# Turned probabilities copied ahead of the next exponentials, in four attention stages of one fused kernel

## What is computed

```
p = softmax(scale * q k^T [+ mask])      # over the keys
o = p v
```

## Time and profile before

| what | value |
|---|---|
| median of three runs | 4049.82 us |
| the profiled execution, its own time | 4044.61 us |
| its span (first to last instruction) | 4042.6 us |
| TensorE (PE) matmuls busy | 3677.2 us, 91% |
| VectorE (DVE) busy | 1608.9 us, 40% |
| ScalarE (ACT) busy | 1214.8 us, 30% |
| DMA | 76 GB/s over the span |
| mean granted TensorE clock | 0.947 of 2.4 GHz |
| the four attention stages | 614 to 648, 1278 to 1491, 1646 to 1680, 3359 to 3572 us |

### The profile page before, as it was taken

The page is one execution under the profiler, slowest core; times in us unless marked ns, Lnnn a source line. Parts: engine busy times, 40 slices in busy tenths (PEclk is TensorE's granted clock), DMA queues, the critical chain, the costliest instruction groups (busy, mean ns, idle before and its releaser), DMA issues. The chain is left out here.

```text
span 4042.6 us, 44686 instructions
## 1 busy us (share of the span) xinstructions
PE 3677.2 (91%) x17866; PEld 2787.5 (69%) x17866; DVE 1608.9 (40%) x2661; ACT 1214.8 (30%) x2127; POOL 169.1 (4%) x282
## 2 busy tenths in 40 slices
PE   7879798999999989999987999799999888888999
PEld 5448677778665667778866745488887645666777
DVE  5343334333403543343334532344433435544443
ACT  3122224222213542332233110322222435533222
POOL 0033010100000001010000000000000011000000
PEclk9779899999999979999998999899999999998999
DMA  3325331222311003122220201111112300011222
GB/s 147 137 108 226 115 125 63 84 83 104 118 42 42 1 11 125 63 84 87 100 101 31 93 0 42 42 63 62 62 52 94 127 21 22 1 42 63 83 73 104
DMA packets 30052, 307.72 MB, mean 76 GB/s; under 512 B 3843, under 2 KB 5604, under 8 KB 9157
## 3 DMA queue, kind: packets, MB, share of 16 engines
q1 hardware_dynamic: 29894, 305.52, 20.3%
HBM read 303.41 MB, written 2.10 MB: 76 GB/s over the span
## 5 line engine op out<-in xcount | busy, mean ns | idle before, releaser
L561 PE MATMUL psum<-operand_rounded,weights_rest 128*128 128x512 f32 (+1 forms) x1360 | 522.3, 384 | 59.7 <-DVE operand_rest L532 59.7
L562 PE MATMUL psum<-operand_rounded,weights_rounded 128*128 128x512 f32 (+1 forms) x1360 | 519.5, 382 | 0.0
L563 PE MATMUL psum<-operand_rest,weights_rounded 128*128 128x512 f32 (+1 forms) x1360 | 518.8, 381 | 0.0
L530 DVE TENSOR_TENSOR weights_rest<-ring,weights_rounded 128x1024 fp32r<-128x1024 f32 x170 | 208.3, 1225 | 579.2 <-ACT operand_rounded L513 579.2
L326 PE MATMUL psum<-operand_rounded,weights_rest 128*128 128x512 f32 (+1 forms) x1056 | 379.7, 360 | 53.2 <-DVE weights_rest L345 53.1
L327 PE MATMUL psum<-operand_rounded,weights_rounded 128*128 128x512 f32 (+1 forms) x1056 | 377.7, 358 | 0.0
L512 ACT ACTIVATE weights_rounded<-ring 128x1024 fp32r<-128x1024 f32 x170 | 180.1, 1059 | 634.7 <-PE psum L563 567.6
L561 PEld LDWEIGHTS psum<-operand_rounded,weights_rest 128*128 128x128 f32 x1360 | 262.3, 193 | 112.5 <-issue 53.2
L563 PEld LDWEIGHTS psum<-operand_rest,weights_rounded 128*128 128x128 f32 x1360 | 262.0, 193 | 48.2
L562 PEld LDWEIGHTS psum<-operand_rounded,weights_rounded 128*128 128x128 f32 x1360 | 262.3, 193 | 47.6
L326 PEld LDWEIGHTS psum<-operand_rounded,weights_rest 128*128 128x128 f32 x1056 | 200.6, 190 | 90.6 <-issue 60.8
(11 more groups left out here) (430 smaller groups left out, 6155.0 us busy)
## 6 DMA issues: line engine op xcount, KB each, us to landing
ring<-in_ff_w SPq DMA_DIRECT2D x32, 2048.0 KB, 7.7
ring<-in_w_mod SPq DMA_DIRECT2D x24, 2048.0 KB, 7.7
ring<-in_ffn_up SPq DMA_DIRECT2D x22, 2048.0 KB, 7.7
ring<-in_ffn_down SPq DMA_DIRECT2D x33, 1024.0 KB, 4.8
ring<-in_a_w_in SPq DMA_DIRECT2D x4, 2048.0 KB, 11.5
ring<-in_xa_wk SPq DMA_DIRECT2D x4, 2048.0 KB, 7.6
ring<-in_xa_wv SPq DMA_DIRECT2D x4, 2048.0 KB, 7.7
ring<-in_xa_wq SPq DMA_DIRECT2D x4, 2048.0 KB, 7.7
```

Source lines behind the costliest of these rows:

```text
L530: dve.tensor_tensor(parts["weights_rest"][:, r % 2, :], weight_rows(s, r), parts["weights_rounded"][:, r % 2, :].bitcast(F32), ALU.subtrac ...
L561: nc.tensor.matmul(k.bank(m, n), rest, top_in, start=first, stop=False)
L562: nc.tensor.matmul(k.bank(m, n), top, top_in, start=False, stop=False)
L563: mm = nc.tensor.matmul(k.bank(m, n), top, rest_in, start=False, stop=last)
```

## The change

In all four stages ACT's queue in step s takes `copy_turned` first and `exponentials(s)` after it. MLA (`paired`) turns, copies and uses the values one unit later than before (`lag` 3 instead of 2); the cross attentions keep their lag of 2. In the sparse attention, units whose two branches fit one bank together (256 and 128 keys) are turned into one bank and copied by one instruction; the semaphores count parts instead of branches.

```diff
@@ attention @@
-    held = 3 if paired else 2
+    held, lag = (3, 3) if paired else (2, 2)
@@ tensor queue @@
-            for step in range(U + 3):
+            for step in range(U + lag + 1):
                 if step < U:
                     score(step)
-                if 2 <= step < U + 2:
-                    turn(step - 2)
-                if step >= 3:
-                    values(step - 3)
+                if lag <= step < U + lag:
+                    turn(step - lag)
+                if step > lag:
+                    values(step - lag - 1)
@@ scalar queue @@
-            for step in range(U + 2):
+            for step in range(U + lag):
+                if step >= lag:
+                    copy_turned(step - lag)
                 if step < U:
                     exponentials(step)
-                if step >= 2:
-                    copy_turned(step - 2)
@@ vector queue @@
-            for step in range(U + 4):
+            for step in range(U + lag + 2):
                 if step < U:
                     maximum(step)
                 if 1 <= step <= U:
                     normalise(step - 1)
-                if step >= 4:
-                    copy_head(step - 4)
+                if step >= lag + 2:
+                    copy_head(step - lag - 2)
@@ sparse_attention @@
+    def in_parts(u):
+        return [(0,), (1,)] if 2 * width_of(u) > BANK else [(0, 1)]
+
+    first_part = [0]
+    for u in range(U):
+        first_part.append(first_part[-1] + len(in_parts(u)))
@@ turn @@
-                for b in range(B):
-                    n = B * u + b
+                for i, branches in enumerate(in_parts(u)):
+                    n, col = first_part[u] + i, 0
                     if n >= 2:
                         pe.wait_ge(*t_copied.at(n - 1))
-                    for at in range(0, width_of(u), P):
-                        mm = nc.tensor.transpose(k.bank(4 + n % 2)[:, at:at + P], probs[...], k.c("ident"))
+                    for b in branches:
+                        for at in range(0, width_of(u), P):
+                            mm = nc.tensor.transpose(k.bank(4 + n % 2)[:, col:col + P], probs[...], k.c("ident"))
+                            col += P
                     mm.then_inc(t_ready.sem, 1)
@@ copy_turned @@
-                for b in range(B):
-                    act.wait_ge(*t_ready.at(B * u + b + 1))
-                    nc.scalar.activation(turned[:, u % held, b * BANK:b * BANK + n], k.bank(4 + (B * u + b) % 2, n), ACT.Copy).then_inc(t_copied.sem, 1)
+                for i, branches in enumerate(in_parts(u)):
+                    part, c = first_part[u] + i, len(branches)
+                    act.wait_ge(*t_ready.at(part + 1))
+                    dst = turned[:, u % held, branches[0] * BANK:(branches[0] + c) * BANK].rearrange("p (b n) -> p b n", b=c)[:, :, 0:n]
+                    src = k.bank(4 + part % 2, c * n).rearrange("p (b n) -> p b n", b=c)
+                    nc.scalar.activation(dst, src, ACT.Copy).then_inc(t_copied.sem, 1)
@@ scalar queue @@
             for step in range(U + lag):
+                if step >= lag:
+                    copy_turned(step - lag)
                 if step < U:
                     exponentials(step)
-                if step >= lag:
-                    copy_turned(step - lag)
```

More of the change, by code:

```diff
@@ L1004, in turn @@
                 pe.wait_ge(*p_norm.at(u + 1))
-                for b in range(B):
-                    n = B * u + b
+                for i, branches in enumerate(in_parts(u)):
+                    n, col = first_part[u] + i, 0
                     if n >= 2:
                         pe.wait_ge(*t_copied.at(n - 1))
-                    for at in range(0, width_of(u), P):
-                        mm = nc.tensor.transpose(k.bank(4 + n % 2)[:, at:at + P], probs[:, u % (lag + 1), b * BANK + at:b * BANK + at + P], k.c("ident"))
+                    for b in branches:
+                        for at in range(0, width_of(u), P):
+                            mm = nc.tensor.transpose(k.bank(4 + n % 2)[:, col:col + P], probs[:, u % (lag + 1), b * BANK + at:b * BANK + at + P], k.c("ident"))
+                            col += P
                     mm.then_inc(t_ready.sem, 1)
@@ L1025, in pair_values @@
             def pair_values(u):
-                pe.wait_ge(*t_copied.at(B * (u + 1)))
+                pe.wait_ge(*t_copied.at(first_part[u + 1]))
                 if u >= 5:
@@ L1048, in exponentials @@
                 if u > lag:
-                    act.wait_ge(*t_ready.at(B * (u - lag)))
+                    act.wait_ge(*t_ready.at(first_part[u - lag]))
                 for b in range(B):
@@ L1105, in sparse_attention @@
     p_step.base += 2 * U
-    t_ready.base += B * U
-    t_copied.base += B * U
+    t_ready.base += first_part[-1]
+    t_copied.base += first_part[-1]
     o_ready.base += U // 2
```

## The result

The changed kernel takes 3976.81 us in the median of four executions (3971.57 to 3989.14), beside 4049.82 us for the kernel before in the same comparison. That is the median of its three ordinary executions; a fourth took 18019.41 us for a reason that no trace shows, and with it the recorded median would be 4051.13. The medians differ by 73 us. The recorded ratio is 0.9829, with a 95% interval of 0.9814 to 0.9843, which makes it 69 us, between 64 and 75, where 65.6 were forecast.

What follows compares the result with a forecast made beforehand. PE was taken to wait on an order of work, not a rate. Savings of 30 + 21 + 12.6 + 1.5 + 0.5 = 65.6 us from 4049.8 gave 3984 us, range 3975 to 3993, chance 0.55.

Steps and rivals of the forecast that it cites:

- ACT's queue closing a loop: MLA and wide sparse units: turn, copy, exponentials, normalising within one step, 10 us more in MLA, about 4064 us; chance 0.03.
- Rivals 2 and 3: Sparse turn keeps another wait, 4019 us, chance 0.04; turns in both stages released by something else, 4050 us, chance 0.02.
- MLA, 30 us forecast: MLA: copy first and lag 3 remove PE's waits for ACT's copies; 30 us saved, between 24 and 33.
- The pair of starts: MLA: summed start distances give 5.55 us for a pair of units without the wait, where it takes 6.53 us.
- the price of a wait: MLA: each wait costs 0.98 us, against 0.79 recorded; 30 of them make 29.4 us.
- The ends: MLA's start and end: lag 3 costs about 0.5 us at the start and gains 1.5 us at the end.
- The third step of lag: MLA: makes room for normalising, which ended at 3407.39 where an unwaiting turn would want its data at 3407.26.
- The sparse waits, 21 us forecast: Sparse attention: new ACT order removes 26 waits, 16.8 us recorded; 21 us saved with 0.16 us surplus each.
- The clock, 12.6 + 1.5 us forecast: Last 16 sparse units: clock stays up, pairs take 2.9 instead of 5.42 us, 12.6 us; the end 1.5 more.
- rival 1: Clock falls in the narrow sparse units as before; 52.5 us saved in all, 3997 us; chance 0.36.
- One bank, nothing forecast: Narrow sparse units: one copy for two spares ACT 0.17 us at most at 256 keys; costed at nothing.
- Cross attentions, 0.5 us forecast: Cross attentions: PE is full in the middle; 0.5 us for both, from the first and last units.

Runs made afterwards that it cites:

- sparse_order_two_banks: Kernel before with only the sparse attention's ACT order changed to copies first, each branch in its own bank; 4015.26 us, ratio 0.9921.
- before_narrow_new: Kernel before with copies first only in the last 16 sparse units; 4032.41 us, ratio 0.9951.
- sparse_one_bank_old_order: Kernel before with only narrow sparse units in one bank and a merged copy, exponentials still first; 4033.53 us, ratio 0.9963.
- after_narrow_old: Changed kernel with the old order and two banks put back in the last 16 sparse units; 3985.52 us, ratio 0.984.
- mla_lag3_old_order: Kernel before with only MLA's lag raised to 3, exponentials still first; 4048.16 us, ratio 0.9998.
- mla_order_lag2: Kernel before with ACT's new order in the dense attentions, MLA's lag kept at 2, sparse attention unchanged; 4022.24 us, ratio 0.9939.
- dense_change_only: Changed kernel with the old sparse attention put back; 4018.11 us, ratio 0.992.
- after_third: Changed kernel, unedited, run again for one more recorded execution; 3981.63 us.

## Why the prediction was right

**The bound.** That PE waited on an order and not on a rate held: with nearly the same work on all engines the three kinds of stage lost 69 us. The one priced rival on the slower side, ACT's queue closing a loop, did not appear; no wait of the scores for exponentials came behind a stage's first units. Rivals 2 and 3, a turn that something else releases, fell with the waits: all 26 of the sparse attention went and 30 of MLA's 31, and nothing took their place inside the stages.

**MLA, 30 us forecast, 31.7 measured.** The pair of starts was right to 0.01 us (5.55 and 5.56), and so was the price of a wait: 30 x (6.53 - 5.56) = 29.1. The ends gave 2.6 where I had 1.0. The head did cost a new short wait (0.32 us). The tail gave more, 1.3 of it for a reason that I had not seen: in the trace of before the clock fell in the last two units, and the values that take 1.53 us took 2.25. That was this execution's and not the change's, since three other traces of the unchanged code keep 1.00 there; beside their 211.0 the change gave 30.4. The timeline of the kernel before:

```profile
3565.78 2.25 PE L867 MATMUL psum<-arena 128*64 128x128 f32 x24
3567.96 1.54 PE L849 MATMUL psum<-const,arena 128*128 128x128 f32 x6
3570.08 1.53 PE L867 MATMUL psum<-arena 128*64 128x128 f32 x24 [0.58 <-ACT arena L899]
```

**The third step of lag.** The step that gave it the job of making room for the normalising held, and its size is now known: 7.4 us with the new order, 0.6 with the old. From the start times I had the normalising late by 0.13 us a pair; it was 0.22. What the trace of before could not show is that lag without order is worth nothing that the runs can tell.

**The sparse waits, 21 us forecast.** The wide units have 23 of the 26 waits and gave 19.0 us; the other three, at 0.83 each, make 2.5. Sum 21.5. The surplus of a wait over its record, 0.16 to 0.19 us, is confirmed in both stages. It pays to measure it from starts: by recorded idle alone MLA and this stage would have come out at 24 and 16.8.

**The clock, 12.6 + 1.5 us forecast.** The pairs of the narrow units now take 2.87 us, where 2.9 was taken. PE's timeline of the changed kernel, beside the earlier trace rows:

```profile
1434.72 0.49 PE L1007 MATMUL psum<-arena 65*128 65x128 f32 x2
...
1436.31 0.41 PE L1019 MATMUL psum<-const,arena 128*128 128x128 f32 x2
...
1437.59 0.49 PE L1007 MATMUL psum<-arena 65*128 65x128 f32 x2
```

The narrow order gave 17.4 us; less 2.5 for its three waits at full clock, 14.9 are the clock and the end, against 14.1. So rival 1 fell, six times of six: the four traces of the changed kernel, sparse_order_two_banks and before_narrow_new. With the narrow waits gone the clock has not been seen to fall there.

My reason for it is only half borne out. I leaned on "it fell just when the waits took their largest share, and those waits go". But sparse_one_bank_old_order and after_narrow_old keep waits in the narrow units and keep 1.00, the first while PE idles for 3.3 of 20 us. The untouched sparse attention itself ran in four traces: in two, before and mla_lag3_old_order, the clock fell near 1456, and in the two others, mla_order_lag2 and dense_change_only, it had fallen early, near 1281, and then held until 1478. The same instructions with the same waits, then, fall in one place in one execution and in another in the next. Two windows of mla_order_lag2 show it:

```profile
1458.00:1478.00 20.00, 16.24 (x157) 13.17 (x156) 11.93 (x55) 11.65 (x62) 0.00 (x0) 1.00 0.01 2
...
1480.00:1482.00 2.00, 2.00 (x13) 1.21 (x13) 1.57 (x8) 1.49 (x9) 0.00 (x0) 0.50 0.00 0
```

PE idles there for 3.8 of 20 us at 1.00, more than the 3.4 ahead of the fall in the earlier trace rows, and this stretch comes after the place at which the clock fell in before. Waits in both halves of the stage were present wherever it fell at 1456, but what decides it is open: with one trace of each of these kernels a fall that comes in some executions only can't be excluded for them. I did not try waits of another length in the same places.

That the size came out at 14.9 is in part luck. It holds between executions without the early fall (212.1 and 175.7). The unchanged stage also took 209.9 us, in the two traces with the early fall, and the changed one 181.1 in its two: between these the stage gained 28.7. Of that the 30 waits of the unchanged stage (19.6 us recorded) make 24.9 at 0.83 each, which leaves 3.8 us for the clock and the end and not 14.1. Over four traces of each the stage went from 211.0 to 178.4, by 32.6 us where 35.1 were forecast.

The Trainium skill ("TensorE: Matmul & The Clock Gate", section "What's actually happening") has activity release the throttle. Here the windows of narrow units show PE busy 20.00 of 20.00 us at 1.00 in after_third, and 26.00 of 26.00 at 0.50 in the earlier trace rows, with the same products at the same widths but for the pair of 256 keys that the first window begins in; the busy share does not tell the two apart. The same page's "A second HAM failure mode: psum-queue depth-cycling" would have the fall go when the short idles go. That agrees with the six traces, but eight such idles in after_narrow_old and 31 in the whole stage of sparse_one_bank_old_order did not bring it, so here the rule is not enough by itself.

**One bank, nothing forecast.** Right beside the new order (176.0 and 175.7). The row of ACT's copies at 256 elements shows what merging does to them:

```profile
L1075 ACT ACTIVATE arena<-psum 128x256 f32<-128x256 f32 x16 | 6.2, 388 | 5.4 <-PE psum L1019 5.4
```

One strided copy of both branches takes 388 ns, as long as a plain one of 256 elements (386 ns), so the view costs nothing; ACT had the time anyway.

**Cross attentions, 0.5 us forecast, 0.95 measured.** mla_order_lag2 and dense_change_only show the same 0.5 us each, so it is the order.

**The sum.** Forecast 65.6; the stages gave 69.1: 1.7 more in MLA, 1.3 in the sparse attention and 0.45 in the cross attentions. That the profiled execution came out within 0.1 us of the 3979.0 forecast for it is chance, since the stages gained 3.5 more and the untouched stretches gave 3.4 of it back. The time, 3976.81 us, is 7 under the 3984 that I gave. It lies in the stated range, but the range's lower end, 3975, does not come out of its own terms: 3 us for MLA, 1 for the narrow pairs and 1.5 for the end lead to 3978.7, and the time is below that. Over 11 executions of the changed kernel the time runs from 3971.57 to 3989.14; the forecast lies inside that spread, and I had not foreseen that it would be wider than that of the kernel before (4044.6 to 4052.6, but for the one of 18019.41).

## What to carry to other kernels

Where PE waits for an evacuation that its engine has stacked behind another unit's exponentials, look at what those exponentials wait for: if it is a later reduction, put the evacuation first. That is worth far more than a deeper lag, and a deeper lag is worth something only once the order is right (here 24 us, then 7; the lag alone, with three slots of `probs`, nothing). Price each wait by the distance of starts with and without it, not by its recorded idle, and list the waits of the weight loads too, since a turn held for its data shows there. Check such a mark against the end of the work that it names: it fitted in one run here and not in another. A term that rests on the clock of one trace wants a second trace of the kernel before.

## What the runs showed that I had not expected

- The clock of the same instructions fell in different places in different executions: near 1281 and 1478, or near 1456. A single trace of before was thin ground for a term of 12.6 us, though it came true.
- A fall at the widest sparse units, in 14 us where PE is busy throughout, cost 5.4 us and appears in two of four traces of the changed kernel, and in two of four of those with the unchanged sparse attention.
- The one-bank part was worth 15.9 us with the old order, though its trace shows more waits than that of before (31 of 17.0 us, against 26 of 16.8): what an edit is worth by itself and what it adds to another can differ by a clock level.
